# A recurrence over chunks, taken in two halves of two head pairs

## The chip, the core and the metric

The kernel is one program on one core of a Trainium2 chip. The engines named here are TensorE (PE in the trace; PEld is its weight load), VectorE (DVE), ScalarE (ACT), GpSimd (POOL) and the DMA queues (SP issues the loads of weights). They run side by side and wait for each other through semaphores. The metric is the device time of one execution in microseconds. The median of three runs of the kernel before is 1818.2 us (1816.91 to 1818.48).

## The reference

A two-layer decoder trunk for 512 tokens of width 1024. Each layer projects the normed input once, feeds three token mixers, adds their gated sum to the stream, and ends in a feed-forward block of width 4096. One of the mixers is a gated DeltaNet with 8 heads of 64 keys and 64 values, in 8 chunks of 64 tokens. The part that matters here is its loop over the chunks:

```python
def step(state, inp):
    q_i, k_i, u_i, w_i, a_i, g_i = inp
    v_new = u_i - jnp.einsum('bhck,bhkv->bhcv', w_i, state)
    o = (jnp.einsum('bhck,bhkv->bhcv', q_i * jnp.exp(g_i)[..., None], state)
         + jnp.einsum('bhcs,bhsv->bhcv', a_i, v_new))
    g_last = g_i[..., -1]
    state = (state * jnp.exp(g_last)[..., None, None]
             + jnp.einsum('bhck,bhcv->bhkv', k_i * jnp.exp(g_last[..., None] - g_i)[..., None], v_new))
    return state, o
```

## The kernel before

All matrix products with weights are done in three passes of 128x512 products (lines 444 to 446, `passes`): high times high, low times high, high times low. The weights come as a stream of 1024-column units; SP loads each, POOL splits it into a high and a low part (lines 407 and 412), and PE multiplies it with a ring of four units between them. `project(tile)` is 8 steps of three such products.

The recurrence is `recur(step)` for step 0 to 8 in each layer (lines 680 to 730). The 8 heads are 4 pairs: the even head of each pair lies on partitions 0 to 63 of the tile `state`, the odd head on 64 to 127. The odd heads run one chunk behind the even ones, so that a step holds chunk `step` of the even and chunk `step - 1` of the odd heads, and steps 0 and 8 hold one parity only. A step is this sequence on PE, in program order (each PE group is 4 pairs x 2 parities = 8 products of 64x64, which the trace shows as 16 instructions, two for each f32 product; where only one parity takes part it is 4 and 8):

1. L692: state times weighted keys, into bank S(2), columns 0 to 255. It waits for `state_done`.
2. One of the 8 steps of the projection tile `av 1`: three 128x512 products (L444 to L446). In step 8 four transposes of the output stand here (L748).
3. L702: the inverse (`gated[...,0,...]`) times the remainder `r`, into S(2), columns 256 to 511. It waits for `r_ready`.
4. L714: state times query, the first part of the chunk's output. It waits for `o_copied` of an earlier step.
5. L724: keys times the new values, the update of the state, into bank S(3). It waits for `vnew_done`. Step 8 has no update.
6. L738: the second part of the chunk's output, from the new values.

Between them DVE subtracts product 1 from the right side to make `r` (L1745, one instruction for each parity), scales the state by its decay (`sdec`, L1750), and adds product 5 to it (L1762; L1764 is the copy that takes its place in step 0). ACT copies product 3 to `vnew` (L1276) and then the output to `o_tm` (L1267). On the same engines, in the same order of program, stand the norm of the outputs: ACT squares them in every second step (L1257), DVE sums the squares in steps 3, 5 and 7 (L1720), and in steps 6 and 8 DVE takes a reciprocal and scales the output (L1724, L1726). In step 0 the first copy to `vnew` stands behind two other copies of ACT (L1250).

Everything is written out by hand: each engine has its own list of instructions, and the semaphores alone tie the lists together. There is no scheduler.

Of the kernel before, what the change touches and what calls it, by code (L numbers as in the profile page):

```python
# [10 lines left out]
ALU = mybir.AluOpType  # L11
# [4 lines left out]
P = 128  # L16
# [7 lines left out]
PAIRS = HEADS // 2  # L24
# [4 lines left out]
CHUNKS = SEQ // CHUNK  # L29
# [23 lines left out]
def chains(step):  # L53

    return [(par, step - par) for par in range(2) if 0 <= step - par < CHUNKS]
# [81 lines left out]
class PerLayer:  # L137
# [18 lines left out]

    lower_done = 4; lower_copied = 4; corner_done = 4; corner_placed = 5

    query_done = 8; ws_done = 8; r_ready = 8; tr_done = 9; vnew_done = 9; supd_done = 8; sdec_done = 7; state_done = 8; o_done = 9; o_copied = 9

    osq_ready = 4; osum_ready = 4; o_root = 4; oinv_ready = 4; on_done = 4; o_token_turned = 4

# [19 lines left out]
def hybrid_trunk(nc, stream, params, x, positions, constants, out):  # L182

    with ExitStack() as ctx:
# [82 lines left out]
        ps = ctx.enter_context(nc.psum_tensor("ps", [P, 8, 512], F32))  # L267
# [88 lines left out]
        per = PerLayer  # L356
# [12 lines left out]
        def turned_probs(h):  # L369

            return probT[:, h % 6] if h % 6 < 4 else probU[:, h % 6 - 4]

        def sums_bank(d):

            return ps[:, 2 + d % 6]
# [57 lines left out]
        def _(pe):  # L433
            pe.wait_ge(ident_in, 16)
            for layer in range(DEPTH):
                mm = nc.tensor.matmul

                def S(n):
                    return ps[:, 2 + n]
# [240 lines left out]
                def recur(step):  # L680

                    both = chains(step)
                    hs = lambda m: np.s_[64 * (m % 2):64 * (m % 2) + 64]
                    cs = lambda par: np.s_[64 * par:64 * par + 64]
                    if step == 0:
                        pe.wait_ge(corner_placed, layer * per.corner_placed + 3)
                    else:
                        pe.wait_ge(state_done, layer * per.state_done + step)
                        for j in range(PAIRS):
                            for par, m in both:  # L690
                                if m:
# [7 lines left out]
                    for j in range(PAIRS):  # L699
                        for par, m in both:  # L700
                            h = 2 * j + par
                            last = mm(S(2)[hs(m), 256 + j * 64:256 + j * 64 + 64], gated[hs(m), m // 2, 0, h],  # L702
                                      r[hs(m), j] if m else rhsv[hs(m), 0, h * 64:h * 64 + 64], start=True, stop=True)
                    last.then_inc(tr_done, 1)
                    if step == 0:
                        project(("av", 1), range(0, 1))
                    if step == 1:
                        pe.wait_ge(corner_placed, layer * per.corner_placed + 5)
                    if step >= 2:
                        pe.wait_ge(o_copied, layer * per.o_copied + step - 1)  # L710
                    for j in range(PAIRS):
                        for par, m in both:
                            if m:
                                last = mm(S(step % 2)[hs(m), j * 64:j * 64 + 64], kqe[cs(par), j, m // 2, m % 2, 1], state[cs(par), j],  # L714
                                          start=j == 0, stop=False, skip_group_check=True)
                    if step:
                        last.then_inc(query_done, 1)
                    pe.wait_ge(vnew_done, layer * per.vnew_done + step + 1)
                    if step < CHUNKS:
                        for j in range(PAIRS):  # L720
                            for par, m in both:
                                if m < CHUNKS - 1:
                                    h = 2 * j + par
                                    last = mm(S(3)[cs(par), j * 64:j * 64 + 64], kend[hs(m), m // 2, h * 64:h * 64 + 64], vnew[hs(m), step % 2, j],  # L724
                                              start=True, stop=True)
                        last.then_inc(supd_done, 1)
# [108 lines left out]
                for t in range(TT):  # L835
                    last = nc.tensor.transpose(S(4)[:, t * ROPE:(t + 1) * ROPE], krT[:, t * P:(t + 1) * P], c("ident", parts=ROPE)[:, 0:ROPE])
# [214 lines left out]
        def _(act):  # L1051
# [48 lines left out]
            for layer in range(DEPTH):  # L1100
                f = nc.scalar.activation

                def S(n):
                    return ps[:, 2 + n]
# [318 lines left out]
        def _(dve):  # L1423
# [84 lines left out]
            for layer in range(DEPTH):  # L1508
                tt_, ts_, stt = nc.vector.tensor_tensor, nc.vector.tensor_scalar, nc.vector.scalar_tensor_tensor

                def S(n):
                    return ps[:, 2 + n]
# [225 lines left out]
                by_pair = lambda t: t.rearrange("p (j v) -> p j v", j=PAIRS)  # L1738
                for step in range(CHUNKS + 1):
                    if step:  # L1740
                        dve.wait_ge(ws_done, layer * per.ws_done + step)
                        for par, m in chains(step):
                            if m:
                                hs = np.s_[64 * (m % 2):64 * (m % 2) + 64]
                                ins = tt_(r[hs], rhsv[hs, m // 2].rearrange("p (j q v) -> p j q v", j=PAIRS, q=2)[:, :, par],  # L1745
                                          by_pair(S(2)[hs, 0:256]), ALU.subtract)
                        ins.then_inc(r_ready, 1)
                    if 0 < step < CHUNKS:
                        dve.wait_ge(state_done, layer * per.state_done + step)
                        tt_(sdec[:], state[:], eglb[:, :, step:step + 1].broadcast_to([P, PAIRS, 64]), ALU.mult).then_inc(sdec_done, 1)  # L1750
                    if step in (3, 5, 7):
                        sum_o((step - 3) // 2)
                    if step in (6, 8):
                        scale_o((step - 6) // 2)
                    if step == CHUNKS:
                        gate_o(0)
                    else:
                        dve.wait_ge(supd_done, layer * per.supd_done + step + 1)
                        if step:
                            rows = np.s_[64:128] if step == CHUNKS - 1 else np.s_[0:128]  # L1760
                            dve.wait_ge(sdec_done, layer * per.sdec_done + step)
                            tt_(state[rows], sdec[rows], by_pair(S(3)[rows, 0:256]), ALU.add).then_inc(state_done, 1)  # L1762
                        else:
                            nc.vector.tensor_copy(state[0:64], by_pair(S(3)[0:64, 0:256])).then_inc(state_done, 1)  # L1764
                take(avT[:, 1], ("av", 1))
                scale_o(2)
                gate_o(1)
# [325 lines left out]
```

## Time and profile before

| | us |
|---|---|
| median of 3 runs | 1818.2 |
| the profiled execution | 1818.84 |
| its span | 1817.0 |
| PE busy in the span | 1795.3 |
| DVE busy | 851.2 |
| ACT busy | 466.5 |
| POOL busy | 1030.7 |

The granted clock of TensorE was 0.999 over the span. The span is what the trace covers; the profiled execution's own time lies 1.84 us above it. The duration of a PE instruction in the trace goes from its start to the arrival of its result, and the next one starts before that: 128x512 products start 0.23 us apart and each lasts 0.39 us. So for PE the distance between two starts tells what an instruction costs, and its end tells when a consumer can go on.

### The profile page before, as it was taken

The page shows a single profiled execution, that of the slowest core. Times are in us where ns is not written, and L with a number is a line of the kernel's source. Part 1 is how long each engine was busy: PE and PEld are TensorE (multiplying, and loading weights), DVE is VectorE, ACT ScalarE, POOL GpSimd, SP SyncE. Part 2 cuts the span into 40 slices and gives each one's busy share as a digit, 9 for nine tenths or more (in the row PEclk, how much of TensorE's full clock was granted, in tenths as well). Part 3 has the DMA queues.
Part 4 walks back from the last instruction along what each step waited for, and adds up shares of the span by engine and source line. Part 5 has one row for each costly group of instructions (what it writes and reads, how often), then busy time and mean ns, then how long its engine had stood idle before and what let it go on. Part 6 is the DMA issues. An engine that isn't in the chain of part 4 may idle for free.

```text
span 1817.0 us, 26580 instructions
## 1 busy us (share of the span) xinstructions
PE 1795.3 (99%) x10182; PEld 1468.6 (81%) x10182; DVE 851.2 (47%) x1391; ACT 466.5 (26%) x904; POOL 1030.7 (57%) x580
## 2 busy tenths in 40 slices
PE   8999999999999999999999999999999999999998
PEld 7887788778888888888878878887888888888887
DVE  8685536654454231314275955366535351414141
ACT  6423316551123000000254232165311130001010
POOL 6544366245666666666664434661556666666672
PEclk9999999999999999999999999999999999999999
DMA  6222133122233233332342211321322322332332
GB/s 232 93 69 71 40 101 105 36 105 87 91 101 107 93 99 98 93 104 94 94 141 67 76 54 59 97 89 36 127 83 93 104 94 93 95 103 93 97 100 70
DMA packets 46761, 167.29 MB, mean 92 GB/s; under 512 B 5018, under 2 KB 8346, under 8 KB 46146
## 3 DMA queue, kind: packets, MB, share of 16 engines
q1 hardware_dynamic: 44066, 154.50, 26.9%
q10 hardware_dynamic: 2592, 11.29, 1.7%
q8 instruction: 81, 1.33, 0.3%
q14 instruction: 22, 0.18, 0.0%
HBM read 159.47 MB, written 6.29 MB: 91 GB/s over the span
## 4 chain that ended last, share of the span: by engine, by line
PE 93%; DVE 4%; ACT 1%; issue 1%; DMA 0%; POOL 0%; SPq 0%; ACTq 0%; DVEq 0%; POOLq 0%
PE ps L444 27%; PE ps L446 27%; PE ps L445 27%; PE ps L922 2%; PE ps L944 1%; PE ps L931 1%; DVE acc L1455 1%; PE ps L692 1%; PE ps L724 1%; PE ps L702 1%; DVE r L1745 1%; DVE hLo L1448 0%; PE ps L605 0%; PE ps L994 0%; PE ps L550 0%
## 5 line engine op out<-in xcount | busy, mean ns | idle before, releaser
L412 POOL TENSOR_TENSOR wLo<-wraw,wHi 128x1024 fp32r<-128x1024 f32 x288 | 722.4, 2509 | 23.8
L407 POOL TENSOR_SCALAR wHi<-wraw 128x1024 fp32r<-128x1024 f32 x288 | 308.3, 1071 | 734.4 <-PE ps L446 718.6
L444 PE MATMUL ps<-hHi,wHi 128*128 128x512 f32 x1360 | 554.6, 408 | 0.5 <-DVE convd L1574 0.5
L446 PE MATMUL ps<-hHi,wLo 128*128 128x512 f32 x1360 | 530.6, 390 | 0.0
L445 PE MATMUL ps<-hLo,wHi 128*128 128x512 f32 x1360 | 530.3, 390 | 0.0
L444 PEld LDWEIGHTS ps<-hHi,wHi 128*128 128x128 f32 x1360 | 255.8, 188 | 59.3 <-issue 6.0
L445 PEld LDWEIGHTS ps<-hLo,wHi 128*128 128x128 f32 x1360 | 256.2, 188 | 55.4 <-issue 4.6
L446 PEld LDWEIGHTS ps<-hHi,wLo 128*128 128x128 f32 x1360 | 255.7, 188 | 54.5
L444 PE MATMUL ps<-fHi,wHi 128*128 128x512 f32 x640 | 249.3, 389 | 0.0
L446 PE MATMUL ps<-fHi,wLo 128*128 128x512 f32 x640 | 249.0, 389 | 0.0
L445 PE MATMUL ps<-fLo,wHi 128*128 128x512 f32 x640 | 249.0, 389 | 0.0
L1405 ACT ACTIVATE fHi<-relu 128x512 fp32r<-128x512 f32 x64 | 40.6, 635 | 555.3 <-DVE relu L1954 555.3
L1968 DVE TENSOR_TENSOR xT<-xT,ps 128x512 f32<-128x512 f32 x56 | 38.5, 687 | 254.8 <-PE ps L446 254.8
L446 PEld LDWEIGHTS ps<-fHi,wLo 128*128 128x128 f32 x640 | 120.1, 188 | 25.0
L445 PEld LDWEIGHTS ps<-fLo,wHi 128*128 128x128 f32 x640 | 120.2, 188 | 25.0
L444 PEld LDWEIGHTS ps<-fHi,wHi 128*128 128x128 f32 x640 | 120.1, 188 | 24.7
L1954 DVE SCALAR_TENSOR_TENSOR relu<-ps,rstdT 128x512 f32<-128x512 f32 x64 | 44.3, 692 | 193.7 <-PE ps L446 185.8
L1120 ACT ACTIVATE sg<-ps 128x512 f32<-128x512 f32 x48 | 28.8, 600 | 256.4 <-DVE ps L1517 256.4
L1517 DVE TENSOR_TENSOR ps<-ps,rstdT 128x512 f32<-128x512 f32 x56 | 38.9, 699 | 114.0 <-PE ps L446 113.8
L446 PE MATMUL ps<-bHi,wLo 128*128 128x512 f32 x192 | 74.7, 389 | 0.0
L444 PE MATMUL ps<-bHi,wHi 128*128 128x512 f32 x192 | 74.7, 389 | 0.0
L445 PE MATMUL ps<-bLo,wHi 128*128 128x512 f32 x192 | 74.7, 389 | 0.0
(310 smaller groups left out, 1955.7 us busy)
## 6 DMA issues: line engine op xcount, KB each, us to landing
wraw<-stream SPq DMA_DIRECT2D x288, 512.0 KB, 3.5
out<-xT ACTq DMA_DIRECT2D x2, 2048.0 KB, 10.0
xT<-out ACTq DMA_DIRECT2D x2, 2048.0 KB, 8.6
xin<-x SPq DMA_DIRECT2D x4, 512.0 KB, 6.2
out<-ost ACTq DMA_DIRECT2D x1, 1024.0 KB, 4.1
out<-ost ACTq DMA_DIRECT2D x2, 512.0 KB, 3.8
prm<-params ACTq DMA_DIRECT2D x1, 647.0 KB, 4.0
prm<-params SPq DMA_DIRECT2D x1, 576.0 KB
```

The lines of the kernel that those rows point to most:

```text
L407: nc.gpsimd.tensor_scalar(wHi[:, slot], wraw[:, slot % RAW], 1.0, 0.0, ALU.mult, ALU.add).then_inc(unit_high, 1)
L412: nc.gpsimd.tensor_tensor(wLo[:, slot], wraw[:, slot % RAW], wHi[:, slot].bitcast(F32), ALU.subtract).then_inc(unit_split, 1)
L444: mm(o, lh[lc], rh[rc], start=start, stop=False)
L445: mm(o, lh[lc], rl[rc], start=False, stop=False)
L446: return mm(o, ll[lc], rh[rc], start=False, stop=stop)
L692: last = mm(S(2)[hs(m), j * 64:j * 64 + 64], kqe[cs(par), j, m // 2, m % 2, 0], state[cs(par), j], start=True, stop=True)
L922: mm(bank[:, 0:w], qhT[0:QK, h, i * P:w], khT[0:QK, h, 0:w], start=True, stop=True).then_inc(score_done, 1)
L1120: f(gate[:, d % 2], bank_of(TILE_NO[tile]), ACT.Sigmoid).then_inc(bank_read[TILE_NO[tile] % 2], 1)
L1405: f(fHi[q % 2][:, n], relu[:, n % 2], ACT.Square).then_inc(f_hi, 1)
L1517: return tt_(o, bank_of(TILE_NO[tile]), rstdT[:], ALU.mult)
L1954: stt(relu[:, n % 2], bank_of(n), 0.0, rstdT[:], ALU.max, ALU.mult).then_inc(relu_done, 1)
L1968: tt_(xT[:, d], xT[:, d], sums_bank(d), ALU.add).then_inc(x_added, 1)
```

## The change

Products 1, 3 and 5 of each step, and what DVE and ACT do with them, are taken in two halves: pairs 0 and 1, then pairs 2 and 3. Each half has its own increment and its own wait of `ws_done`, `r_ready`, `tr_done`, `vnew_done`, `supd_done` and `state_done`. The results of the first half go to bank 4 and those of the second to bank 5 (`half_bank`), each with columns 0 to 127 for product 1, 128 to 255 for product 3 and 256 to 383 for product 5. (Before, bank 4 held products 1 and 3 of all pairs and bank 5 product 5.) The decay (`sdec`), the two output products and the output copies stay whole. The `sdec` instruction waits for both halves of the state.

```diff
-    query_done = 8; ws_done = 8; r_ready = 8; tr_done = 9; vnew_done = 9; supd_done = 8; sdec_done = 7; state_done = 8; o_done = 9; o_copied = 9
+    query_done = 8; ws_done = 16; r_ready = 16; tr_done = 18; vnew_done = 18; supd_done = 16; sdec_done = 7; state_done = 16; o_done = 9; o_copied = 9
...
+        def half_bank(half, part):
+
+            return ps[:, 4 + half, part * P:(part + 1) * P]
...
-                        pe.wait_ge(state_done, layer * per.state_done + step)
-                        for j in range(PAIRS):
-                            for par, m in both:
-                                if m:
-                                    last = mm(S(2)[hs(m), j * 64:j * 64 + 64], kqe[cs(par), j, m // 2, m % 2, 0], state[cs(par), j], start=True, stop=True)
-                        last.then_inc(ws_done, 1)
+                        for half in range(2):
+                            pe.wait_ge(state_done, layer * per.state_done + 2 * step - 1 + half)
+                            for j in (2 * half, 2 * half + 1):
+                                for par, m in both:
+                                    if m:
+                                        last = mm(half_bank(half, 0)[hs(m), j % 2 * 64:j % 2 * 64 + 64], kqe[cs(par), j, m // 2, m % 2, 0], state[cs(par), j],
+                                                  start=True, stop=True)
+                            last.then_inc(ws_done, 1)
...
-                        pe.wait_ge(r_ready, layer * per.r_ready + step)
...
+                    for half in range(2):
+                        if step:
+                            pe.wait_ge(r_ready, layer * per.r_ready + 2 * step - 1 + half)
+                        for j in (2 * half, 2 * half + 1):
...
+                        last.then_inc(tr_done, 1)
...
-                    pe.wait_ge(vnew_done, layer * per.vnew_done + step + 1)
...
+                    for half in range(2):
+                        pe.wait_ge(vnew_done, layer * per.vnew_done + 2 * step + half + 1)
+                        if step < CHUNKS:
+                            for j in (2 * half, 2 * half + 1):
...
+                            last.then_inc(supd_done, 1)
...
-                    act.wait_ge(tr_done, layer * per.tr_done + step + 1)
-                    nc.scalar.copy(vnew[rows, step % 2].rearrange("p j v -> p (j v)"), S(2)[rows, 256:512]).then_inc(vnew_done, 1)
+                    for half in range(2):
+                        act.wait_ge(tr_done, layer * per.tr_done + 2 * step + half + 1)
+                        nc.scalar.copy(vnew[rows, step % 2, 2 * half:2 * half + 2].rearrange("p j v -> p (j v)"), half_bank(half, 1)[rows]).then_inc(vnew_done, 1)
...
-                        dve.wait_ge(ws_done, layer * per.ws_done + step)
...
+                        for half in range(2):
+                            pairs = np.s_[2 * half:2 * half + 2]
+                            dve.wait_ge(ws_done, layer * per.ws_done + 2 * step - 1 + half)
...
+                                    ins = tt_(r[hs, pairs], rhsv[hs, m // 2].rearrange("p (j q v) -> p j q v", j=PAIRS, q=2)[:, pairs, par],
+                                              by_pair(half_bank(half, 0)[hs]), ALU.subtract)
+                            ins.then_inc(r_ready, 1)
                     if 0 < step < CHUNKS:
-                        dve.wait_ge(state_done, layer * per.state_done + step)
+                        dve.wait_ge(state_done, layer * per.state_done + 2 * step)
...
-                            tt_(state[rows], sdec[rows], by_pair(S(3)[rows, 0:256]), ALU.add).then_inc(state_done, 1)
...
+                                tt_(state[rows, pairs], sdec[rows, pairs], by_pair(half_bank(half, 2)[rows]), ALU.add).then_inc(state_done, 1)
```

On PE no instruction is added or moved; the waits between them are. The rows below are PE's list in step 2 of layer 0, before: product 1, the projection step and product 3.

```order
L692 MATMUL ps<-state,kqe 64x64 [waits state_done]
L692 MATMUL ps<-state,kqe 64x64 x7
L444 MATMUL ps<-hHi,wHi 128x512
L445 MATMUL ps<-hLo,wHi 128x512
L446 MATMUL ps<-hHi,wLo 128x512
L702 MATMUL ps<-r,gated 64x64 [waits r_ready]
L702 MATMUL ps<-r,gated 64x64 x7
```

The same place after the change (lines 692, 444 to 446 and 702 have become 697, 448 to 450 and 710):

```order
L697 MATMUL ps<-state,kqe 64x64 [waits state_done]
L697 MATMUL ps<-state,kqe 64x64
L697 MATMUL ps<-state,kqe 64x64 [waits state_done]
L697 MATMUL ps<-state,kqe 64x64 x3
L448 MATMUL ps<-hHi,wHi 128x512
L449 MATMUL ps<-hLo,wHi 128x512
L450 MATMUL ps<-hHi,wLo 128x512
L710 MATMUL ps<-r,gated 64x64 [waits r_ready]
L710 MATMUL ps<-r,gated 64x64 x3
L710 MATMUL ps<-r,gated 64x64 [waits r_ready]
L710 MATMUL ps<-r,gated 64x64 x3
```

The group of 8 has become two of 4 with a wait ahead of each; what stands between the groups is as it was. Product 5 (L724, now L733) is cut in the same way.

DVE's list in the same step, before: the remainder, the decay, the update of the state, and the next step's first instruction.

```order
L1745 TENSOR_TENSOR r<-rhsv,ps 64x256 [waits ws_done]
L1745 TENSOR_TENSOR r<-rhsv,ps 64x256
L1750 TENSOR_TENSOR sdec<-state,eglb 128x256 [waits state_done]
L1762 TENSOR_TENSOR state<-sdec,ps 128x256 [waits sdec_done,supd_done]
L1745 TENSOR_TENSOR r<-rhsv,ps 64x256 [waits ws_done]
```

And after:

```order
L1757 TENSOR_TENSOR r<-rhsv,ps 64x128 [waits ws_done]
L1757 TENSOR_TENSOR r<-rhsv,ps 64x128
L1757 TENSOR_TENSOR r<-rhsv,ps 64x128 [waits ws_done]
L1757 TENSOR_TENSOR r<-rhsv,ps 64x128
L1762 TENSOR_TENSOR sdec<-state,eglb 128x256 [waits state_done]
L1776 TENSOR_TENSOR state<-sdec,ps 128x128 [waits sdec_done,supd_done] x2
L1757 TENSOR_TENSOR r<-rhsv,ps 64x128 [waits ws_done]
```

Two remainder instructions of 256 columns have become four of 128, and one state update has become two; the decay still stands between them, whole.

## Rows read from the trace of the kernel before

**Rows 1.** The page: busy time by engine, and the chain by engine.

```profile
PE 1795.3 (99%) x10182; PEld 1468.6 (81%) x10182; DVE 851.2 (47%) x1391; ACT 466.5 (26%) x904; POOL 1030.7 (57%) x580
...
PE 93%; DVE 4%; ACT 1%; issue 1%; DMA 0%; POOL 0%; SPq 0%; ACTq 0%; DVEq 0%; POOLq 0%
```

**Rows 2.** Timeline of step 2, layer 0: start us, us, instruction, count [idle before].

```profile
176.15 0.68 PE L692 MATMUL ps<-state,kqe 64*64 64x64 f32 x16 [0.23 <-DVE state L1762]
176.76 0.50 PE L444 MATMUL ps<-hHi,wHi 128*128 128x512 f32 x1
176.88 0.85 DVE L1745 TENSOR_TENSOR r<-rhsv,ps 64x256 f32<-64x256 f32 x2 [0.78 <-PE ps L692]
177.10 0.40 PE L445 MATMUL ps<-hLo,wHi 128*128 128x512 f32 x1
177.33 0.40 PE L446 MATMUL ps<-hHi,wLo 128*128 128x512 f32 x1
177.79 0.68 PE L702 MATMUL ps<-r,gated 64*64 64x64 f32 x16
178.30 0.63 PE L714 MATMUL ps<-state,kqe 64*64 64x64 f32 x16
178.52 0.37 ACT L1276 COPY vnew<-ps 128x256 f32<-128x256 f32 x1 [1.80 <-PE ps L702]
178.94 0.68 PE L724 MATMUL ps<-vnew,kend 64*64 64x64 f32 x16
179.46 0.63 PE L738 MATMUL ps<-vnew,gated 64*64 64x64 f32 x16
179.67 0.42 DVE L1762 TENSOR_TENSOR state<-sdec,ps 128x256 f32<-128x256 f32 x1 [1.48 <-PE ps L724]
180.15 0.68 PE L692 MATMUL ps<-state,kqe 64*64 64x64 f32 x16
```

**Rows 3.** Timeline, layer 0: where steps 0, 1, 7 and 8 start.

```profile
169.31 0.67 PE L702 MATMUL ps<-rhsv,gated 64*64 64x64 f32 x8
...
170.63 0.37 ACT L1276 COPY vnew<-ps 64x256 f32<-64x256 f32 x1
...
172.30 0.67 PE L692 MATMUL ps<-state,kqe 64*64 64x64 f32 x8
...
196.12 0.68 PE L692 MATMUL ps<-state,kqe 64*64 64x64 f32 x16
...
200.09 0.68 PE L692 MATMUL ps<-state,kqe 64*64 64x64 f32 x8 [0.22 <-DVE state L1762]
...
202.58 0.65 PE L738 MATMUL ps<-vnew,gated 64*64 64x64 f32 x8
```

**Rows 4.** Timeline of PE: from a 128x512 product to a small one.

```profile
167.86 0.39 PE L446 MATMUL ps<-hHi,wLo 128*128 128x512 f32 x1
168.18 1.20 PE L674 MATMUL ps<-gated,lower 32*32 32x32 f32 x64
```

**Rows 5.** Groups by shape: short instructions that read PSUM (count, busy us, mean ns).

```profile
L1745 DVE TENSOR_TENSOR r<-rhsv,ps 64x256 f32<-64x256 f32 x28 | 11.7, 420 | 12.6 <-PE ps L692 12.5
L1881 DVE COPY probT<-ps 128x128 f32<-128x128 f32 x12 | 3.5, 292 | 4.0 <-PE ps L931 4.0
L1276 ACT COPY vnew<-ps 128x256 f32<-128x256 f32 x14 | 5.2, 372 | 20.4 <-PE ps L702 20.4
L1223 ACT COPY lsums<-ps 128x128 f32<-128x128 f32 x2 | 0.6, 283 | 0.0
```

**Rows 6.** Timeline of step 6, layer 0: DVE's other work before the state.

```profile
194.31 0.69 DVE L1726 TENSOR_TENSOR o_tm<-o_tm,ostat 128x512 f32<-128x512 f32 x1
195.64 0.42 DVE L1762 TENSOR_TENSOR state<-sdec,ps 128x256 f32<-128x256 f32 x1 [0.64 <-PE ps L724]
```

**Rows 7.** Timeline behind the recurrence, layer 0: the one wait of PE.

```profile
212.03 1.65 DVE L1726 TENSOR_TENSOR o_tm<-o_tm,ostat 128x512 f32<-128x512 f32 x1
213.74 0.65 PE L748 MATMUL ps<-cst,o_tm 128*128 128x128 f32 x4
```

More of the change, by code:

```diff
@@ L697, in recur @@
                             turn_delta_output(0)
-                        pe.wait_ge(r_ready, layer * per.r_ready + step)
[L699 to L704, printed above, removed]
+                    for half in range(2):
+                        if step:
+                            pe.wait_ge(r_ready, layer * per.r_ready + 2 * step - 1 + half)
+                        for j in (2 * half, 2 * half + 1):
+                            for par, m in both:
+                                h = 2 * j + par
+                                last = mm(half_bank(half, 1)[hs(m), j % 2 * 64:j % 2 * 64 + 64], gated[hs(m), m // 2, 0, h],
+                                          r[hs(m), j] if m else rhsv[hs(m), 0, h * 64:h * 64 + 64], start=True, stop=True)
+                        last.then_inc(tr_done, 1)
                     if step == 0:
@@ L717, in recur @@
                         last.then_inc(query_done, 1)
-                    pe.wait_ge(vnew_done, layer * per.vnew_done + step + 1)
[L719 to L726, printed above, removed]
+                    for half in range(2):
+                        pe.wait_ge(vnew_done, layer * per.vnew_done + 2 * step + half + 1)
+                        if step < CHUNKS:
+                            for j in (2 * half, 2 * half + 1):
+                                for par, m in both:
+                                    if m < CHUNKS - 1:
+                                        h = 2 * j + par
+                                        last = mm(half_bank(half, 2)[cs(par), j % 2 * 64:j % 2 * 64 + 64], kend[hs(m), m // 2, h * 64:h * 64 + 64],
+                                                  vnew[hs(m), step % 2, j], start=True, stop=True)
+                            last.then_inc(supd_done, 1)
                     if step == 0:
@@ L1737, in _ @@
                 dve.wait_ge(z_ready, layer * per.z_ready + 4)
-                by_pair = lambda t: t.rearrange("p (j v) -> p j v", j=PAIRS)
+                by_pair = lambda t: t.rearrange("p (j v) -> p j v", j=2)
                 for step in range(CHUNKS + 1):
                     if step:
-                        dve.wait_ge(ws_done, layer * per.ws_done + step)
[L1742 to L1747, printed above, removed]
+                        for half in range(2):
+                            pairs = np.s_[2 * half:2 * half + 2]
+                            dve.wait_ge(ws_done, layer * per.ws_done + 2 * step - 1 + half)
+                            for par, m in chains(step):
+                                if m:
+                                    hs = np.s_[64 * (m % 2):64 * (m % 2) + 64]
+                                    ins = tt_(r[hs, pairs], rhsv[hs, m // 2].rearrange("p (j q v) -> p j q v", j=PAIRS, q=2)[:, pairs, par],
+                                              by_pair(half_bank(half, 0)[hs]), ALU.subtract)
+                            ins.then_inc(r_ready, 1)
                     if 0 < step < CHUNKS:
-                        dve.wait_ge(state_done, layer * per.state_done + step)
+                        dve.wait_ge(state_done, layer * per.state_done + 2 * step)
                         tt_(sdec[:], state[:], eglb[:, :, step:step + 1].broadcast_to([P, PAIRS, 64]), ALU.mult).then_inc(sdec_done, 1)
@@ L1757, in _ @@
                     else:
[L1758 to L1761, printed above, removed]
-                            tt_(state[rows], sdec[rows], by_pair(S(3)[rows, 0:256]), ALU.add).then_inc(state_done, 1)
-                        else:
-                            nc.vector.tensor_copy(state[0:64], by_pair(S(3)[0:64, 0:256])).then_inc(state_done, 1)
+                        for half in range(2):
+                            pairs = np.s_[2 * half:2 * half + 2]
+                            dve.wait_ge(supd_done, layer * per.supd_done + 2 * step + half + 1)
+                            if step:
+                                rows = np.s_[64:128] if step == CHUNKS - 1 else np.s_[0:128]
+                                dve.wait_ge(sdec_done, layer * per.sdec_done + step)
+                                tt_(state[rows, pairs], sdec[rows, pairs], by_pair(half_bank(half, 2)[rows]), ALU.add).then_inc(state_done, 1)
+                            else:
+                                nc.vector.tensor_copy(state[0:64, pairs], by_pair(half_bank(half, 2)[0:64])).then_inc(state_done, 1)
                 take(avT[:, 1], ("av", 1))
```

## The prediction

> **What bounds the kernel now.** I read the page first: PE is busy for 1795.3 of 1817.0 us and holds 93% of the chain, DVE 4% [rows 1]. So there is nothing to win but PE's few idle stretches, and little to lose but new ones. The list of waits puts most of PE's small idle in the recurrence, so I read the timeline of one full step next [rows 2]. It is a closed loop. Counted from the start of product 1 (176.15):
>
> - product 1 lasts until 0.68; DVE starts 0.05 later and makes the remainder in 0.85, until 1.58;
> - PE has meanwhile issued product 1 (0.61) and the projection step, whose third product starts at 1.18. It could go on at about 1.50 (below), but product 3 starts at 1.64, when the remainder is there;
> - product 3 has arrived at 2.32, ACT copies from 2.37 to 2.74, and product 5 starts at 2.79. The query product fills PE only until about 2.59;
> - product 5 has arrived at 3.47, DVE writes the state from 3.52 to 3.94, and the next product 1 starts at 4.00. The output product fills PE until about 3.75.
>
> So three gaps, 0.14, 0.20 and 0.25 us, in a step of 4.00 us. PE's rows show each as a small number or none, because a result's flight (0.22 us behind the last start) counts as busy; the gaps must be read from the starts. The pattern stands 12 times, in steps 2 to 7 of both layers: layer 0 takes 23.94 us for six of them, from 176.15 to 200.09 [rows 2, 3], which is 3.99 each. Step 0 takes 2.99 us, step 1 3.85 us, and step 8 2.49 us up to its output product [rows 2, 3].
>
> **What PE alone would take for a step.** Product 1 with the switch to the wide products 0.61 (176.15 to 176.76), two distances between wide products 0.57 (to 177.33), and 0.32 from a wide product to a small one, where nothing waits [rows 4]. Products 3 and query: from 177.79 to the last query start, 178.30 + 0.63 - 0.22 = 178.71, and one distance of 0.03 on, is 0.95; products 5 and output in the same way 0.96 (178.94 to 179.90) [rows 2]. Sum: 0.61 + 0.57 + 0.32 + 0.95 + 0.96 = 3.41 us. Nothing in the change adds or removes a PE product, so this is the floor of a full step, and 0.58 us below the 3.99 of now.
>
> **What the halves cost.** A product group of 16 trace instructions takes some 0.46 to 0.48 to issue and 0.68 to arrive, so a half is issued in 0.24 and has arrived after 0.45. No row shows a wait inside a group. A wait that is already satisfied costs nothing between two groups: query follows product 3 after 0.51 and output follows product 5 after 0.52, each over a wait [rows 2]. I take 0 for it; the other end is 0.22 each, if a half had to arrive before the next one is issued.
>
> DVE: no row has a remainder of 128 columns. 256 columns of 64 partitions take 0.42, a PSUM copy of 128 columns 0.292 [rows 5]. The ends are 0.21 (half of 0.42) and 0.42 (no shorter at all); I take 0.29, the row that has the width. Four remainders then take 1.16 instead of 0.85, two state updates 0.58 instead of 0.42. ACT: 256 columns take 0.372, 128 columns 0.283 [rows 5]; I take 0.28, the ends are 0.19 and 0.37.
>
> **The step after the change**, from its first product 1 on:
>
> - product 1: half one 0 to 0.24, arrived at 0.45; half two arrived at 0.68;
> - remainders from 0.50: half one is ready at 1.08 + 0.06, half two at 1.66 + 0.06 = 1.72;
> - product 3: half one at 1.50, PE's own time; half two at 1.74, just covered. First gap gone;
> - ACT: half one arrived at 1.95, copied 2.00 to 2.28; half two arrived 2.19, copied 2.28 to 2.56, ready 2.61;
> - query ends its issue at 2.45; product 5 at 2.45 and 2.69, both covered. Second gap gone;
> - output 2.93 to 3.41; state half one from 2.95 (2.90 + 0.05) to 3.24, half two from 3.24 to 3.53, ready 3.58. The next product 1 needs them at 3.41 and 3.65. Third gap gone, with 0.07 left.
>
> So the loop comes down to PE's 3.41, but with slack of only 0.02, 0.08 and 0.07 at the second halves. The decay (0.42, whole) follows the remainders at 1.66 and ends at 2.08, well before 2.95. In step 6 the reciprocal and the scaling follow: the scaling ended 0.64 us before the state before [rows 6], at 195.00 or 2.88 of its step, and with remainders that end 0.08 later at about 2.97, which pushes the state by some 0.1. In steps 3, 5 and 7 only the sum of squares stands there, one instruction in place of two, and ends earlier.
>
> The sum for a layer: full steps 23.94 - 6 x 3.41 = 3.48, less 0.10 for step 6. Step 1 3.85 - 3.41 = 0.44. In step 0 ACT can't start the first copy before 170.63 in either case [rows 3]; its half two is ready at 170.63 + 0.56 + 0.05 = 171.24 instead of 171.04, but product 5 half two has then arrived at 171.69, its state is ready at 172.08, and PE, done with the output product at about 171.95, starts product 1 there instead of at 172.30: 0.35. In step 8 the second remainder comes at 1.18, product 3 is issued until 1.50 and arrives at 1.71, ACT's second copy is ready at 2.14 instead of 2.49: 0.35. Together 3.48 - 0.10 + 0.44 + 0.35 + 0.35 = 4.52, in two layers 9.0 us.
>
> Nothing takes it back behind the recurrence by what I see: the next work is PE's own, the units of weights are split well ahead (POOL is busy 57% [rows 1]), and PE's only wait there, 0.3 us for a scaling that took 1.65 us [rows 7] where the same instruction takes 0.69 [rows 6], may grow or go by its length, since DVE's and PE's lists shift against each other: +-0.5 us in all. The profiled execution took 1818.84 us, of which 1817.0 are span; less 9.0 it is 1809.8. The median of the runs is 0.64 below the profiled execution, so 1809.2 us.
>
> A rule that speaks against splitting stands in the Trainium skill, TensorE: Matmul & The Clock Gate, section "The cost: per-tile semaphore tail": increments by matmuls serialize, and each adds about 26 ns to the tail. The trace has groups with one increment only, which DVE follows 0.05 us after arrival, and so can't say. By the rule, as an estimate, three more increments in each of 14 steps (1 to 7) would cost 14 x 3 x 0.026 = 1.1 us, and the time would be 1810.3.
>
> **Rivals.**
>
> *The second half is late (chance 0.20).* The slack of the second halves is 0.02 to 0.08 us, and it goes if the short instructions of DVE and ACT are longer than their nearest rows. With DVE's at 0.36, midway to 0.42, the last remainder is ready at 2.00, product 3's second half starts 0.26 late, product 5's second half is pushed to 2.95 by PE and ACT, and the state's second half (arrival 3.40, + 0.05 + 0.36 + 0.05) comes at 3.86, or 3.62 for the start of the next product 1. That leaves 0.37 of 0.58 a step: 5.8 us in all, 1813 us. At the end 0.42 the step comes to 3.9 and about 1 us is left: 1817.5. With ACT alone at 0.37, the second copy is ready 0.10 late: 1.2 us in 12 steps, 1810.4. For it: instructions with two short runs of 64 and a step between them are in no row at this width. Against it: the remainder of 256 columns has the same form and costs what plain ones do.
>
> Here the Trainium skill, VectorE: DVE Perf Modes, section on the TRN2 errata, advises tiles of at least 512 elements, since each instruction pays a fixed cost. Its formula, (N+151)/0.96 ns, would give 291 ns for 128 columns as an estimate, the same as the row; by it the price of the split is paid and the sum stays 1809.2.
>
> *The halves bring PE nothing (0.11).* If a wait inside a group makes PE let its results arrive before it goes on, each of the three costs 0.22 us, and 3 x 0.22 = 0.66 eats the 0.58: 1818 to 1819 us. For it: no row shows a satisfied wait inside a product group. Against it: the waits between groups cost nothing.
>
> *Slower (0.06).* The same three places, with a restart on top of the flight: 0.22, and the 0.09 by which the start of a small product behind a wide one (0.32) lies above the distance of wide ones (0.23) [rows 2, 4], are 0.31 us at each, 0.93 a step against 0.58 won, so 14 x 0.35 = 4.9 us more: 1823 us. It decides from 0.19 us at each place. Against it: small products follow small ones at 0.03 in every group, and no mode is switched inside one.
>
> The forecast itself (1807 to 1812) has 0.63. What is left is gain smaller than 0.2% or more for causes I don't see.
>
> **Numbers.** 0.2% is 3.6 us, about what a measurement of this kernel can tell from no change. Faster by more: the forecast 0.63 and nearly all of the first rival, 0.81. Within: 0.13, the rest of that rival and the second one. Slower: 0.06. The range reaches down to 1807 (the sum, a wait less behind the recurrence and a run's scatter of 1.6 us) and up to 1815, into the first rival; beyond it lie the 0.42 end and the other two.
>
> **What would show it.** In the profile after: starts of product 1 some 3.4 us apart in steps 2 to 7; four remainders of about 0.29 from 0.50 after the start of product 1; the query product, product 5 and the output product without a gap; PE's waits for the remainder and for `vnew` nearly gone in the list of waits. DVE instructions of 0.4, starts 3.8 us apart, or a step between the two halves of a group on PE would show the sum wrong; and if the recurrence is 9 us shorter and the span is not, the work behind it would have to show new waits.

## The result, and the profile after

| | before | after |
|---|---|---|
| median, us | 1816.91 (5 runs) | 1807.02 (5 runs, 1805.79 to 1807.12) |
| ratio | | 0.9936, 95% interval 0.9925 to 0.9948 |
| span of the profiled execution, us | 1817.0 | 1805.2 |
| step 0's first product to the first wide product behind step 8, layer 0 | 34.25 | 28.55 |

By the ratio the change made the kernel 0.64% faster; a second measurement gave 1806.84 against 1818.40 us, ratio 0.9934 (0.992 to 0.9947). The forecast was 9.0 us, the ratio is worth 11.6. By it the time of the 1818.2 us kernel comes to 1806.6, below the range, which began at 1807.0. The times alone place this only roughly: the interval of the ratio reaches from 9.5 to 13.6 us, and the two medians of the table lie 9.9 us apart. What fixes the size is the trace, below. The direction was right and the size too small.

The last row of the table is the measure used below, the **stretch** of a recurrence, from these rows (before, then after; the row of before where it starts is in [rows 3]):

```profile
203.56 0.47 PE L444 MATMUL ps<-hHi,wHi 128*128 128x512 f32 x1
```
```profile
168.65 0.68 PE L710 MATMUL ps<-rhsv,gated 64*64 64x64 f32 x8
...
197.20 0.47 PE L448 MATMUL ps<-hHi,wHi 128*128 128x512 f32 x1
```

It is the same within 0.01 us in both layers and both profiled executions of the changed kernel, while what stands ahead of the first recurrence scatters: step 0 begins at 169.31 us before, and at 168.65, 168.95 and up to 170.4 us in later profiles with the same work ahead of it. Two recurrences won 2 x 5.70 = 11.4 us of the 11.8 between the two spans. The rest is 0.66 us of earlier start of the first recurrence, less 0.3 us that the work behind the two recurrences takes longer.

The page of after, busy time, to be set beside [rows 1]:

```profile
PE 1788.3 (99%) x10182; PEld 1466.3 (81%) x10182; DVE 858.8 (48%) x1435; ACT 468.7 (26%) x922; POOL 1031.1 (57%) x580
```

PE has the same 10182 instructions. Product 1 of step 2 is 16 of them in both kernels; the list in "The change" shows only two of the four products of its first half. PE's busy time fell by 7.0 us for the same work, since the flight of a result (0.22 us from the last start to its arrival) counts as busy and PE now issues during it. DVE is 7.6 us busier with 44 more instructions, ACT 2.2 us with 18 more, and both are cheap: their engines wait anyway. The timeline of step 2 (start us, us, instruction) answers to [rows 2]:

```profile
174.31 0.68 PE L697 MATMUL ps<-state,kqe 64*64 64x64 f32 x16
174.81 1.20 DVE L1757 TENSOR_TENSOR r<-rhsv,ps 64x128 f32<-64x128 f32 x4 [0.32 <-PE ps L697]
174.93 0.50 PE L448 MATMUL ps<-hHi,wHi 128*128 128x512 f32 x1
175.51 0.40 PE L450 MATMUL ps<-hHi,wLo 128*128 128x512 f32 x1
175.83 0.68 PE L710 MATMUL ps<-r,gated 64*64 64x64 f32 x16
176.33 0.50 ACT L1286 COPY vnew<-ps 128x128 f32<-128x128 f32 x2 [1.08 <-PE ps L710]
176.35 0.63 PE L722 MATMUL ps<-state,kqe 64*64 64x64 f32 x16
176.81 0.63 PE L733 MATMUL ps<-vnew,kend 64*64 64x64 f32 x16
177.26 0.52 DVE L1776 TENSOR_TENSOR state<-sdec,ps 128x128 f32<-128x128 f32 x2 [0.79 <-PE ps L733]
177.28 0.52 PE L747 MATMUL ps<-vnew,gated 64*64 64x64 f32 x12
177.60 0.28 PE L697 MATMUL ps<-state,kqe 64*64 64x64 f32 x2
177.63 0.28 PE L747 MATMUL ps<-vnew,gated 64*64 64x64 f32 x4
```

Three things are to be seen. DVE starts 0.50 us after product 1 instead of 0.73, ACT 0.50 after product 3, DVE again 0.45 after product 5. PE goes from group to group at 0.52, 0.46 and 0.47. And in the last two rows the next step's product 1 begins while the output product is not yet issued. The last is what the forecast lacked, and step 3 shows more of it:

```profile
179.11 0.52 PE L710 MATMUL ps<-r,gated 64*64 64x64 f32 x10
...
179.40 0.27 PE L722 MATMUL ps<-state,kqe 64*64 64x64 f32 x2
...
179.60 0.51 ACT L1286 COPY vnew<-ps 128x128 f32<-128x128 f32 x2 [0.23 <-PE ps L710]
...
179.92 0.52 PE L733 MATMUL ps<-vnew,kend 64*64 64x64 f32 x10
...
180.22 0.27 PE L747 MATMUL ps<-vnew,gated 64*64 64x64 f32 x2
...
180.76 0.69 PE L697 MATMUL ps<-state,kqe 64*64 64x64 f32 x16
```

Query starts 0.29 behind product 3, output 0.30 behind product 5. Product 5 starts 0.81 behind product 3; in step 2 it was 0.98. Steps 2 to 7 take 3.29, 3.16, 3.29, 3.15, 3.37 and 3.14 us: 19.40 together instead of 23.94.

The groups by shape, to be set beside [rows 5]:

```profile
L1757 DVE TENSOR_TENSOR r<-rhsv,ps 64x128 f32<-64x128 f32 x56 | 15.8, 286 | 5.8 <-PE ps L697 5.1
L1776 DVE TENSOR_TENSOR state<-sdec,ps 128x128 f32<-128x128 f32 x24 | 6.2, 287 | 6.7 <-PE ps L733 6.6
L1286 ACT COPY vnew<-ps 128x128 f32<-128x128 f32 x28 | 7.1, 266 | 10.7 <-PE ps L710 10.7
```

And the waits of the weight loads in the recurrence (total us, times, longest):

```profile
PEld ps L710 <- DVE r L1757: 4.0, 12, 0.4
PEld ps L733 <- ACT vnew L1286: 1.0, 2, 0.5
```

The first row looks like a wait for the remainder, 0.33 us each. It is none: the first half of the remainder is there at about 175.4, and product 3 starts at 175.83, 0.32 behind the last wide product, which is the distance of [rows 4], where nothing waits. The weight load of product 3 starts only with the product, as after every such switch here, and the list puts the idle time down to the nearest semaphore. The wait for the state is gone from the list, the one of product 5 for the new values stands only in step 0.

### The profile page after: what moved, and what is told of

The parts are those of the page before. It is cut to its first block, busy times and chain, and to the rows that moved or that the text cites. A ratio compares the mean times of both kernels' runs of the same rounds, so it can differ in the third digit from the quotient of the medians.

```text
span 1805.2 us, 26656 instructions
## 1 busy us (share of the span) xinstructions
PE 1788.3 (99%) x10182; PEld 1466.3 (81%) x10182; DVE 858.8 (48%) x1435; ACT 468.7 (26%) x922; POOL 1031.1 (57%) x580
## 4 chain that ended last, share of the span: by engine, by line
PE 95%; DVE 3%; ACT 1%; issue 1%; DMA 0%; POOL 0%; SPq 0%; ACTq 0%; DVEq 0%; POOLq 0%
PE ps L448 28%; PE ps L450 27%; PE ps L449 27%; PE ps L931 2%; PE ps L953 1%; PE ps L940 1%; DVE acc L1465 1%; DVE hLo L1458 1%; PE ps L710 0%; PE ps L609 0%; PE ps L697 0%; PE ps L747 0%; PE ps L1003 0%; PE ps L733 0%; PE ps L722 0%
```

## The experiments

**One junction made whole at a time, and all three.** The changed kernel has three places where PE waits in halves. Each of these kernels keeps both halves of every instruction, but one wait of PE (in the fourth all three) is for the second half already:

```diff
-                            pe.wait_ge(r_ready, layer * per.r_ready + 2 * step - 1 + half)
+                            pe.wait_ge(r_ready, layer * per.r_ready + 2 * step)
```
```diff
-                        pe.wait_ge(vnew_done, layer * per.vnew_done + 2 * step + half + 1)
+                        pe.wait_ge(vnew_done, layer * per.vnew_done + 2 * step + 2)
```
```diff
-                            pe.wait_ge(state_done, layer * per.state_done + 2 * step - 1 + half)
+                            pe.wait_ge(state_done, layer * per.state_done + 2 * step)
```

> The changed kernel, but PE waits for both halves of the remainder before it starts either half of product 3; all other halves stay. Theory (PE's own list is the bound, and each of the three junctions in halves closes a gap of its own): the remainder takes 1.20 us from 0.50 on, ready at 1.75 of its step, while PE is free at 1.52. So 0.23 us come back in each of steps 2 to 7 (not in steps 1 and 8, where the remainder is two instructions and long done): 12 x 0.23 = 2.8 us of the 11.4 that the two recurrences won. Stretch of a recurrence 28.55 + 1.4 = 29.9 us. Rival (the second and third junction have enough slack to absorb it, the loop is bound by the chain and not by PE): under 1 us. Rival (all of the gain comes from here): 9 us or more.

> The changed kernel, but PE waits for both halves of the new values before product 5 starts. Theory (PE bound, three separate gaps): the second copy of ACT is ready 0.07 us behind PE in even steps, 0.24 in odd ones (where PE issues product 3 and the query product 0.14 faster), 0.16 in step 0: 0.16 + 4 x 0.24 + 3 x 0.07 = 1.3 us a recurrence, 2.7 in all, stretch 29.9 us. If even and odd steps have the same PE floor, as the prediction took it (3.41), both would lose 0.15. Rival (absorbed): under 1 us.

> The changed kernel, but PE waits for both halves of the state before product 1 starts. Theory (PE bound, three separate gaps): the state's second half is ready 0.23 us behind PE's end of the output product in each of steps 1 to 8: 8 x 0.23 = 1.8 us a recurrence, 3.7 in all, stretch 30.4 us. Rival (absorbed): under 1 us.

> All three waits of PE are for both halves; the short instructions of DVE and ACT, their early starts and the banks stay as in the changed kernel. Theory (it is PE's waits in halves that win): a step is 0.50 + 1.20 + 0.05 to product 3, 0.73 to ACT's second copy + 0.32, 0.73 to the state's second half + 0.34: 3.87 us against 3.99 before, so 1.5 to 2 us of the gain are left in both recurrences and the time is some 1.7 us below the kernel before. Rival (the separate banks or the short instructions carry the gain by themselves): 5 us or more left. Rival (the short instructions cost, and only the waits make up for it): slower than before by 1 us or more.

The stretch can be read from two rows of each timeline, PE's first product 3 and the wide product behind the last transposes. The remainder whole, then the state whole:

```profile
170.38 0.67 PE L710 MATMUL ps<-rhsv,gated 64*64 64x64 f32 x8
...
200.28 0.47 PE L448 MATMUL ps<-hHi,wHi 128*128 128x512 f32 x1
```
```profile
170.36 0.67 PE L710 MATMUL ps<-rhsv,gated 64*64 64x64 f32 x8
...
200.72 0.47 PE L448 MATMUL ps<-hHi,wHi 128*128 128x512 f32 x1
```

| whole | stretch, us | expected | more than after, two layers | median, us | ratio to before |
|---|---|---|---|---|---|
| none (after) | 28.55 | | 0 | 1807.02 | 0.9936 |
| remainder | 29.90 | 29.9 | 2.7 | 1810.72 | 0.9956 (0.9939 to 0.9972) |
| new values | 29.93 | 29.9 | 2.8 | 1810.43 | 0.9962 (0.9948 to 0.9976) |
| state | 30.36 | 30.4 | 3.6 | 1812.10 | 0.996 (0.9946 to 0.9974) |
| all three | 33.16 | | 9.2 | 1816.62 | 0.9997 (0.9988 to 1.0007) |

The three stretches lie within 0.04 us of what was expected. Each junction (a place where PE waits for another engine's result) closes a gap of its own, none absorbs another's: 1.35 + 1.38 + 1.81 = 4.54 us, and all three together 4.61. The ratios of the first three can't be told from each other; of the stretches, the state's can be told from the other two, which are alike. With all three whole, a full step was expected at 3.87 us:

```profile
175.28 0.68 PE L697 MATMUL ps<-state,kqe 64*64 64x64 f32 x16
...
177.04 0.68 PE L710 MATMUL ps<-r,gated 64*64 64x64 f32 x16 [0.17 <-DVE r L1757]
...
179.15 0.68 PE L697 MATMUL ps<-state,kqe 64*64 64x64 f32 x16
```

It is 3.87, and 2 x (34.25 - 33.16) = 2.2 of 11.4 us stay, a little more than the 1.5 to 2 expected. The median is 1.8 us below the kernel before, which the interval can't tell from nothing. The halves of DVE and ACT start earlier than the whole did. At product 3 that does not pay for the extra instructions: it starts 1.76 behind product 1, where it was 1.64. At the other two junctions it pays: product 5 comes 1.04 behind product 3 (it was 1.15), and the next product 1 comes 1.07 behind product 5 (it was 1.21). So the banks and the short instructions together are worth 2.2 us, and PE's waits in halves the other 9.2. Here the wait of 0.17 in brackets is real: product 3 comes 0.57 behind the last wide product, which starts at 176.47, and not 0.32.

**Why odd steps are shorter.** The contraction partitions and the output partitions of a small product, 0 to 63 or 64 to 127 each, together name what is called its quadrant of the array here. In even steps all five products lie on the same partitions in and out, quadrants (0,0) and (1,1). In odd steps products 3 and output do, and product 1, query and product 5 cross over, (0,1) and (1,0). The flip moves query's output and nothing else:

```diff
-                                last = mm(S(step % 2)[hs(m), j * 64:j * 64 + 64], kqe[cs(par), j, m // 2, m % 2, 1], state[cs(par), j],
+                                last = mm(S(step % 2)[hs(m + (2 <= step < CHUNKS)), j * 64:j * 64 + 64], kqe[cs(par), j, m // 2, m % 2, 1], state[cs(par), j],
```

> The changed kernel, but in steps 2 to 7 the query product of each head writes its result to the other 64 partitions of its bank, so its output is not the reference's; nothing else moves, neither order nor waits. Contraction partitions and output partitions name a quadrant of the array. In even steps all five products use quadrants (0,0) and (1,1); in odd steps products 3 and output use these, and product 1, query and product 5 use (0,1) and (1,0). Theory (a group of products starts before the one ahead of it has been issued where the two use different quadrants, and this makes odd steps 0.12 shorter): with the flip the query product starts 0.3 us after product 3 in even steps instead of 0.5, and 0.5 instead of 0.3 in odd ones. Even steps come from 3.28 to about 3.1 us (product 5 can move up by 0.17 until ACT's first copy binds), odd ones stay within 0.05 (the query product now overlaps with product 5 instead of product 3). Rival (the overlap comes from the order of the heads or from DVE's and ACT's timing, not from quadrants): both distances stay as they are, 0.51 and 0.29.

Product 3 and the first query of step 2, then of step 3, in the timeline of the flip:

```profile
177.47 0.52 PE L710 MATMUL ps<-r,gated 64*64 64x64 f32 x10
...
177.77 0.27 PE L722 MATMUL ps<-state,kqe 64*64 64x64 f32 x2
177.82 0.23 PE L710 MATMUL ps<-r,gated 64*64 64x64 f32 x2
...
180.65 0.68 PE L710 MATMUL ps<-r,gated 64*64 64x64 f32 x16
...
181.16 0.52 PE L722 MATMUL ps<-state,kqe 64*64 64x64 f32 x12
...
181.46 0.27 PE L733 MATMUL ps<-vnew,kend 64*64 64x64 f32 x2
```

The two distances have changed places: 0.30 in the even step, 0.51 in the odd one, and query now overlaps with product 5. A query product even starts (177.77) before a product 3 that stands ahead of it in the program (177.82). So it is quadrants and not order. Of the even steps, step 2 comes to 3.16 us, step 4 to the expected 3.10, and step 6 to 3.33. The odd steps 3, 5 and 7 take 3.26 to 3.27 instead of 3.14 to 3.16, some 0.06 past the bound I gave: in step 3 it now takes 1.74 us from product 3 to the next product 1 and not 1.65. The two nearly cancel: steps 2 to 7 take 19.38 us instead of 19.40, and the stretch is 28.46. The flip moves the overlap and wins nothing by itself. "Different tiles can execute LdWeights and Matmul in parallel", says the Trainium skill, TensorEngine Tiling (Array Packing), section "Key Properties"; the trace agrees, with 0.21 us between the two distances.

**How near the chain is behind PE.** Two kernels ask it from both sides: one takes work from PE, the projection steps (`project(("av", 1))` whole ahead of the loop, none in it), and one lets PE finish its odd steps earlier, by issuing each pair's query behind its product 3:

```diff
+                    beside_query = step in (3, 5, 7)
...
+                            if beside_query:
+                                asked = query((j,))
```

> The changed kernel, but the projection tile av 1 is issued whole ahead of the recurrence, and its steps don't stand in it. Theory (with halves PE's list and the chain through the second halves are nearly equally long): without the filler product 3 half one starts at 1.15 but half two at 1.75 as before (the fourth remainder), so a step stays 3.1 to 3.3 us, the stretch from the first product 3 to the first wide product behind it 27.5 to 28.5, and the kernel is 9 to 11 us slower than the changed one since the 8 x 0.69 us of each layer are now on top. Rival (PE's list alone is the bound, with slack in the chain): a step shrinks by the 0.9 us of the filler and its two switches, the stretch comes to about 22 us, and the kernel is 2 us faster than the changed one.

> The changed kernel, but in steps 3, 5 and 7 the query product of each pair is issued right behind product 3 of the same pair, since the two use different quadrants there. Theory (PE and the chain bind nearly together: in odd steps product 5 starts at the moment ACT's first copy is ready, 0.32 after the copy's start): filling the quadrants better wins next to nothing, step 3 stays 3.16 within 0.1 us, stretch 28.2 to 28.8. Rival (PE's list alone binds in odd steps): the two groups take 0.5 instead of 0.81 us, each of the three steps gets 0.3 shorter, stretch 27.65, 1.8 us in all. Rival (the query products between the halves delay product 3): 0.1 to 0.2 longer each.

Without the filler, product 3 of step 2 is in two pieces, with a wait ahead of each:

```profile
180.88 0.68 PE L697 MATMUL ps<-state,kqe 64*64 64x64 f32 x16 [0.21 <-DVE state L1773]
...
182.01 0.45 PE L708 MATMUL ps<-r,gated 64*64 64x64 f32 x8 [0.45 <-DVE r L1754]
...
182.63 0.45 PE L708 MATMUL ps<-r,gated 64*64 64x64 f32 x8 [0.17 <-DVE r L1754]
...
184.17 0.27 PE L697 MATMUL ps<-state,kqe 64*64 64x64 f32 x2
```

Step 2 takes 3.29 us and step 3 3.11: with 0.9 us of PE's list taken out, they are 0.00 and 0.05 shorter. The stretch is 27.25 us, 0.25 below what I gave, so the eight projection steps, 5.5 us of work, cost 1.3 us where they stand, 1.16 of it in steps 0 and 1. The kernel takes 1817.88 us in its one run, 11 more than the changed one; 2 of them lie ahead of the recurrence, in the start-up.

With query beside product 3, the pieces of step 3 read:

```profile
179.57 0.27 PE L720 MATMUL ps<-r,gated 64*64 64x64 f32 x2
179.58 0.27 PE L708 MATMUL ps<-state,kqe 64*64 64x64 f32 x2
...
180.06 0.51 ACT L1296 COPY vnew<-ps 128x128 f32<-128x128 f32 x2 [0.23 <-PE ps L720]
...
180.38 0.52 PE L743 MATMUL ps<-vnew,kend 64*64 64x64 f32 x10
```

The 32 instructions of the two groups are issued in some 0.5 us, four for every two of before, yet product 5 starts 0.81 behind product 3 as in the changed kernel: 0.32 behind ACT's start, which is one copy and a semaphore. Stretch 28.56, step 3 3.16. So in odd steps ACT's first copy sets the start of product 5, and issuing PE's products sooner wins nothing there. Even steps are another matter: step 4 of the flip took 3.10 instead of 3.29, so the chain alone would allow about 0.2 us less than PE's list takes there. Whether an order with the right output can use this was not tried.

**Both ends.** Step 8 won nothing in the changed kernel:

```profile
194.92 0.68 PE L710 MATMUL ps<-r,gated 64*64 64x64 f32 x8
195.40 0.49 ACT L1286 COPY vnew<-ps 64x128 f32<-64x128 f32 x2 [0.75 <-PE ps L710]
195.43 0.63 PE L722 MATMUL ps<-state,kqe 64*64 64x64 f32 x8
196.21 0.65 PE L747 MATMUL ps<-vnew,gated 64*64 64x64 f32 x8
```

Product 3 and the output product are 1.29 apart as before. ACT's copies end at 195.89, though the list of waits names ACT for the idle time here. What PE waits for is its own query product (`query_done`), which arrives at 196.06 and which product 5 covers in steps 1 to 7.

```diff
-                    else:
+                    elif step < CHUNKS:
                         pe.wait_ge(query_done, layer * per.query_done + step)
```

> The changed kernel without PE's wait for its own query product ahead of the output product in step 8, the one step with no product 5 between the two. Theory (there this wait, and not ACT's copy, lets the output product start, and took away the 0.35 us that I had expected of step 8): the output product starts some 0.27 us earlier, 1.02 after product 3 instead of 1.29; stretch 28.3 instead of 28.55 us, 0.5 us in all. Rival (ACT's copy binds): 1.29 stays.

```profile
195.40 0.68 PE L710 MATMUL ps<-r,gated 64*64 64x64 f32 x8
195.91 0.63 PE L722 MATMUL ps<-state,kqe 64*64 64x64 f32 x8
196.51 0.65 PE L747 MATMUL ps<-vnew,gated 64*64 64x64 f32 x8
```

1.11 instead of 1.29 and a stretch of 28.39: the wait was the bound, but I had expected 1.02. Product 3, 8 instructions of one head parity, takes 0.51 to issue, as long as 16 of two, which I had left out, and the query product 0.60. Why 0.60 and not 0.51 stays open.

The last kernel has this and, in step 0, ACT's two copies of the new values ahead of its last copy for the inverse:

```diff
+                        if (hf, ch) == (1, 0):
+                            for half in range(2):
+                                act.wait_ge(tr_done, layer * per.tr_done + half + 1)
+                                nc.scalar.copy(vnew[0:64, 0, 2 * half:2 * half + 2].rearrange("p j v -> p (j v)"), half_bank(half, 1)[0:64]).then_inc(vnew_done, 1)
```

> The changed kernel as it is, on another chip and beside the next one. Theory (the gain is the two recurrences, 2 x 5.68 us, and what the single runs scatter beyond it lies ahead of the first recurrence): 11.4 us below the kernel before within the interval, ratio 0.9937; stretch 28.55 us again. Rival (part of the 11.6 was the start-up of that execution): 9 to 10 us, ratio 0.995.

> The changed kernel with both ends of the recurrence mended: no wait for the query product in step 8 (worth 0.16 us of stretch when alone), and in step 0 ACT's two copies of the new values stand ahead of the last of its copies for the inverse instead of behind it. Theory (step 0 is bound by ACT's order: product 5 starts at 1.63 of the step though PE is free at 1.49): product 5 starts at 1.49, 0.14 us earlier, stretch 28.55 - 0.16 - 0.14 = 28.25 us, 0.6 us in all, which the times can hardly tell from the changed kernel (0.03%). Rival (the output product of step 0 then waits for the displaced copy): stretch stays at 28.4.

```profile
169.08 0.67 PE L710 MATMUL ps<-rhsv,gated 64*64 64x64 f32 x8
...
170.58 0.68 PE L733 MATMUL ps<-vnew,kend 64*64 64x64 f32 x8
...
197.34 0.48 PE L448 MATMUL ps<-hHi,wHi 128*128 128x512 f32 x1
```

Product 5 of step 0 starts at 1.50 of the step, and the stretch is 28.26 us (28.25 expected). The repeated changed kernel measured 1806.84 us (1805.49 to 1807.01), this one 1805.18 (1804.75 to 1808.20), ratio to before 0.993 (0.9917 to 0.9944). The stretches say 0.6 us better in both recurrences together; the times overlap and can't tell.

## Why the prediction was right and where it fell short

**What held.** What bound the loop (three gaps of PE in each step) was read rightly. Each of them closed, and the three experiments put a price on each. DVE's half remainder was taken at 0.29 us and measured 0.286, ACT's half copy at 0.28 and measured 0.266. A satisfied wait inside a group costs nothing: in the changed kernel product 3 lasts 0.68 us with a wait in its middle, as it did whole. By that the rivals "the halves bring PE nothing" and "slower" fall. "The second half is late" needed DVE at 0.36; it falls as well. Step 6 was 0.08 longer than steps 2 and 4, for 0.10 forecast. The wait behind the recurrence [rows 7] stayed as it was, with the scaling at 1.66 us and 0.32 of idle time (0.29 before) ahead of the weight load of PE's transposes; between PE's own starts it is only 0.29, against 0.23 where nothing waits.

**What failed is the step "What PE alone would take for a step", 3.41 us, called "the floor of a full step".** The mean was 3.23, and this is 12 x 0.18 = 2.1 us, where 2.4 are missing. I took it from step 2 alone, an even step, and wrote it for all. The timeline of step 3 before had it in plain sight:

```profile
181.78 0.51 PE L702 MATMUL ps<-r,gated 64*64 64x64 f32 x10
182.08 0.27 PE L714 MATMUL ps<-state,kqe 64*64 64x64 f32 x2
```

The query starts 0.30 behind product 3, not 0.51. Before the change this could not be seen in the length of a step, since PE had gaps and all steps were 3.99: overlap on an engine that then waits is worth nothing. With the gaps closed odd steps take 0.25 less than the forecast floor, and even ones 0.12 less, since the output product overlaps there with the next product 1, which uses other quadrants (0.32 instead of 0.47). The flip shows the quadrants to be the cause for the query product; for the output product the same cause is argued from the distances, no run changes them.

**The smaller terms**, for one layer:

| | forecast | measured |
|---|---|---|
| steps 2 to 7 | 3.38 | 4.54 |
| step 1 | 0.44 | 0.70 |
| step 0 | 0.35 | 0.48 |
| step 8 up to its output product | 0.35 | -0.01 |
| sum | 4.52 | 5.71 |

Steps 0 and 1 won 0.39 more than forecast and step 8 0.36 less, so that these errors cancel: that the missing 2.4 us are so near the full steps' share is luck. Step 1 is an odd step and was mis-sized for the same reason. Step 0 is better since two short copies in a row take 0.42 on ACT and 0.48 on DVE, not 0.56 and 0.58. Step 8 is the one place where the mechanism was wrong: I listed the chain through DVE and ACT and forgot PE's wait for its own product, which takes 0.18 of the 0.35. The other 0.17 were not there to be had: without the wait the output product still came 1.11 behind product 3. The sum of the steps and the stretch (5.70) differ by 0.01 us in the last transposes.

Two sums of the prediction are off by a little: a gain of 5.8 us from 1818.2 gives 1812.4, not 1813, and the four chances already add up to 1.00, so that nothing is left for other causes. Neither touches the forecast.

**The rule on increments** of the Trainium skill, TensorE: Matmul & The Clock Gate, section "The cost: per-tile semaphore tail", would have cost 1.1 us by the estimate of the prediction. The trace shows no such thing: DVE starts 0.50 us after product 1, which is 0.23 for half the group, 0.22 of flight and 0.05, with two increments as with one. With eight instructions between two increments, this case says nothing on many increments close together.

## What to carry to other kernels

Where a loop of small dependent stages leaves an engine idle at every hand-over, cut the stages into two independent halves with their own waits: here each of three hand-overs gave 2.7 to 3.6 us, all to be added, and the short instructions took nothing back in sum, on engines that wait anyway. Before forecasting that an engine's own list becomes the bound, read the list of every kind of iteration (here even and odd), since overlap that is worthless beside a gap counts once the gap is closed. And look, at the loop's ends, for waits that the middle of the loop covers.

## What the runs showed of the hardware

- Small matrix products that use different quadrants of the array run at once, and one may start before another that is ahead of it in the program: groups of 16 instructions follow at 0.29 to 0.32 us where the quadrants differ and at 0.46 to 0.52 where they are the same and nothing waits. Issued alternately, 32 of them take about 0.5 us.
- From 64x64 products to a wide product and back, PE pays: in full steps the wide one starts 0.61 to 0.63 behind the start of a group that takes 0.46 to 0.52 otherwise, the next wide one 0.34 behind it instead of 0.23, and the small one 0.32 behind the last wide one.
- When PE waits for its own result, it goes on 0.15 us after that has arrived (196.06 to 196.21 in step 8); DVE and ACT start 0.05 after the arrival of PE's results. The arrivals are the ends that the profile gives, which are modelled.
- The list of waits names DVE for idle time of the weight load that is a switch from wide to small products (0.33 us, 12 times), and ACT for PE's wait for its own query product in step 8 (0.26 us).
